# A hybrid attention layer on one core: the low part of the keys contracts over 64 rows instead of over 128 rows padded with zeros

## The chip, the cores and the metric

The kernel runs on one core of one Trainium2 chip. The metric is the device time of one execution in microseconds (us). TensorE is called PE below, its weight loads PEld, VectorE DVE, ScalarE ACT, GpSimd POOL and SyncE SP.

## What is computed

One decoder layer over 1024 tokens of width 2048, all in float32. A root-mean-square norm feeds one input projection of 6400 columns. Its columns go to two mixers:

```python
# A: 8 heads with two softmax maps each, head size 64, causal, value width 128
sc = einsum('bthcd,bshcd->bhcts', q, k) * 64 ** -0.5      # masked, softmax
a  = p[:, :, 0] - lam * p[:, :, 1]
oa = rmsnorm(einsum('bhts,bshe->bthe', a, v)) * (1 - lam_init) * silu(gate_a)
# B: 16 query heads, 2 key/value heads, window 128, a learned sink per head
ob = softmax([q k^T / 8 in the window, sink])[..., :-1] @ v * silu(gate_b)
out = x + concat(oa, ob) @ w_out
```

Queries and keys of both mixers get a norm per head and rotary angles first.

## The kernel before

**Precision.** Every product that must be close to float32 is made from two parts: a "hi" part, rounded to the matmul's own float32 format (F32R), and a "lo" part, the rest. The projection takes three matmuls for each tile (`three`, L854 to L856: hi·hi, hi·lo, lo·hi).

**Order of the work.** After a start of about 200 us (the norm of x, its transposes, the first two projected tiles) the kernel runs 13 units: 8 heads of A, 4 pairs of query heads of B, and a last one that drains. A unit has 16 steps of the same pattern, and every engine has its own hand-written program for a step (`body`), tied to the others by semaphores. In an even step PE does half a quarter of the next unit's projection (12 matmuls, 128x512), maybe transposes (L891), the second half of the quarter, then scores (`scores_a` with c = 0, or `scores_b`), and the transposes of the probabilities of the step before (L938). In an odd step it does the two halves of the projection with the transpose of an output between them (L974), `scores_a` with c = 1, the products with the values (L953, L955, or L966, L967 for B), and the transposes of the next queries and keys (L984). After the units comes the output projection (from 1640 us on).

**The scores.** A head's queries stand in `q_pair`: the 64 rows of one half (`half_rows[c]`) hold q hi, the 64 rows of the other half hold q lo. `k_dup[c]` holds k hi in both halves, so one matmul over all 128 rows, L897, gives q hi · k hi and q lo · k hi together. The second matmul, L898, adds q hi · k lo. It too runs over 128 rows: `kT_lo[c]` is a plane of its own for each c, with k lo in the half where q hi stands and zeros in the other. For A there are two such planes (planes 6 and 7 of `parts`, the tile called attention_parts in the trace). B uses plane 6 alone, with k lo in both halves, for both of its r; there the half with q hi is the upper one for r = 0 and the lower one for r = 1.

**The zeros.** POOL writes them once, at L1480, after it has made its share of the low part of x, and before the units begin PE waits for them (`k_zeros`). Each A step writes only the 64 rows of `kT_lo[c]` that hold k lo, so the zeros stay; B, which comes last, writes all rows of `kT_lo[0]` and needs none.

**Shapes.** For A and query block i, a map has (i+1)·128 keys, in pieces of at most 512: 1 piece for i below 4, 2 from 4 on. For B a step has 4 pieces of 256 (128 for i = 0). Each piece is one L897 and one L898, with the same 128 columns of `q_pair` as the weights.

**DMA.** All transfers of the trace but the one issued by ACT at the start come from SP's queue; POOL issues none.

Of the kernel before, what the change touches and what calls it, by code (L numbers as in the profile page):

```python
# [32 lines left out]
F32 = mybir.dt.float32  # L33
F32R = mybir.dt.float32r
I32 = mybir.dt.int32
ALU = mybir.AluOpType
# [3 lines left out]
P = 128  # L40
D = 2048
S = 1024
HD = 64
HALF = HD // 2
NR = S // P
# [119 lines left out]
def bank_of(name, first_it):  # L165
    return (BASE[first_it] + uses_of(first_it).index(name)) % 2


def qk_split(i, it, first):


    if i:
        return use_number(("T", i), it, first) + 1
    return BASE[first] + (it - first) * len(uses_of(first))
# [26 lines left out]
def decoder_layer(nc, x, positions, norm_w, w_in, q_norm_a, k_norm_a, lambda_q1, lambda_k1,  # L201
# [14 lines left out]
    with ExitStack() as ctx:  # L216
        def sb(name, shape, dt=F32):
            return ctx.enter_context(nc.sbuf_tensor(name, shape, dt))

        def sem(name):  # L220
            return ctx.enter_context(nc.semaphore(name))
# [9 lines left out]
        with nc.sbuf_tensor("x_raw_sb", [P, 3 * D + 2 * 512], F32) as x_raw_sb:  # L231
# [1 line left out]
            x_pieces = [x_raw_sb[:, 3 * D + j * 512:3 * D + (j + 1) * 512] for j in range(2)]  # L233


        parts = sb("attention_parts", [P, 8, S], F32R)
        k_dup = [parts[:, 0, :], parts[:, 1, :]]
        v_hi, v_lo = (parts[:, c, :].rearrange("p (n e) -> p n e", n=NR) for c in (2, 3))
        aT_hi, aT_lo = parts[:, 4, :], parts[:, 5, :]
        kT_lo = [parts[:, 6, :], parts[:, 7, :]]  # L240


        o_second_b = parts[0:HD, 1, 0:512]
# [2 lines left out]
        q_pair = sb("q_hi_lo", [P, 4 * P], F32R)  # L246
# [37 lines left out]
        p_tmp = ps_b[:, 3, :]  # L284
        half_rows = [slice(0, HD), slice(HD, P)]

        names = """consts k_zeros ident_ready par_in lam_in lam_sum lam_exp pos_in ang rope_arg rope_ready
            x_sq x_pow x_scaled x_hi norm_in
            w_hi_ready w_lo_ready w_used
            tp_done tp_free sq_ready ss_ready norm_chain rs_ready  # L290
# [3 lines left out]
        sm = {n: sem("s_" + n) for n in names}  # L294
# [5 lines left out]
        x_lo = {"dve": sem("s_x_lo_dve"), "pool": sem("s_x_lo_pool")}  # L300
# [25 lines left out]
        def wait(eng, s, value):  # L326

            if isinstance(value, int) and value <= 0:
                return
            eng.wait_ge(s, value)  # L330

        def iterations(eng, body, phases=PHASES):

            body(-1, -1)
            for f, n in phases:
                if n == 1:
                    body(f, f)
                else:
                    with eng.Fori(f, f + n) as it:
                        body(it, f)  # L340
# [510 lines left out]
        def _(pe):  # L851
            def three(dst, a_hi, a_lo, b_hi, b_lo, start, stop):

                pe.matmul(dst, a_hi, b_hi, start=start, stop=False)  # L854
                pe.matmul(dst, a_hi, b_lo, start=False, stop=False)  # L855
                return pe.matmul(dst, a_lo, b_hi, start=False, stop=stop)  # L856
# [30 lines left out]
            def turn_tile(d, b, n, bank):  # L887
                wait(pe, pp_copied[b], d["T"] + 1)
                bank_free(n)
                for r in range(4):  # L890
                    mm = pe.transpose(p_tr[bank][:, r * P:(r + 1) * P], stage[:, b, r * P:(r + 1) * P], ident[:, :])  # L891
                mm.then_inc(sm["tp_done"], 1)

            def q_times_k(dst, q, k, k_lo):


                pe.matmul(dst, q, k, start=True, stop=False)  # L897
                return pe.matmul(dst, q, k_lo, start=False, stop=True)  # L898

            def scores_a(st, c, it, first):  # L900
                i = st["i"]
                w = (i + 1) * P
                if c == 0:

                    wait(pe, sm["tp_free"], qk_split(i, it, first))
                wait(pe, sm["x_done"], st["G"] * 2 + c)
                flat = p_s.rearrange("p a b -> p (a b)")
                for lo in range(0, w, 512):
                    t = slice(lo, min(w, lo + 512))
                    mm = q_times_k(flat[:, t], q_pair[:, c * P:(c + 1) * P], k_dup[c][:, t], kT_lo[c][:, t])  # L910
                mm.then_inc(sm["s_done"], 1)

            def scores_b(st, it, first):
                i = st["i"]
                wait(pe, sm["tp_free"], qk_split(i, it, first))
                wait(pe, sm["x_done"], st["G"] * 2)
                t = slice(max(i - 1, 0) * P, (i + 1) * P)
                lo = P if i == 0 else 0
                for r in range(2):
                    for p in range(2):  # L920
                        mm = q_times_k(p_s[:, r, p * 256 + lo:p * 256 + 256],
                                       q_pair[:, (2 * r + p) * P:(2 * r + p + 1) * P], k_dup[0][:, t], kT_lo[0][:, t])
                    mm.then_inc(sm["s_done"], 1)

            def turn_probs(st, it, first):
# [88 lines left out]
            def body(it, first):  # L1014
                for s in range(16):
# [23 lines left out]
                    if s % 2 == 0:  # L1039
                        if cur and cur["k"] == "A":  # L1040
                            scores_a(cur, 0, it, first)
                        elif cur:
                            scores_b(cur, it, first)
                        if back1:
                            turn_probs(back1, it, first)
                        continue
                    if tb:
                        turn_tile(tb[0], tb[2], use_number(tb[1], it, first), bank_of(tb[1], first))
                    if cur and cur["k"] == "A":
                        scores_a(cur, 1, it, first)  # L1050
# [7 lines left out]
            def first_half_k(q, g):  # L1058

                if g == 0:  # L1060
                    pe.wait_ge(sm["w_lo_ready"], q + 1)
                if q == g == 0:
                    wait_x_lo(pe, 2 * NR - 4)
                    wait_x_lo(pe, 2 * NR - 1)
                w, kk = slice(g * P, (g + 1) * P), 4 * q + g
                return three(p_proj[0], w_hi[:, q, w], w_lo[:, q, w], hT_hi[:, kk, 0:512], hT_lo[:, kk, 0:512],
                             kk == 0, kk == KT - 1)

            pe.wait_ge(sm["ident_ready"], 2)
            for r in range(NR):  # L1070
                pe.wait_ge(sm["x_scaled"], r + 1)
                for g in range(4):
                    n = 4 * r + g
                    wait(pe, sm["tp_free"], n - 3)
                    for k in range(4):
                        f = (4 * g + k) * P
                        mm = pe.transpose(ps_b[:, g, k * P:(k + 1) * P], x_buf[r % 2][:, f:f + P], ident[:, :])
                    mm.then_inc(sm["tp_done"], 1)
                    q = r - NR // 2 - 1
                    if q >= 0:  # L1080
                        mm = first_half_k(q, g)
            for g in range(4):
                mm = first_half_k(3, g)
# [3 lines left out]
            for s in range(8):  # L1087
# [3 lines left out]
                quarter(KV_TILES[u], u, s % 4, 1, KV_TILES[0] if u else None)  # L1091
                if 4 <= s < 6:
                    turn_tile(KV_TILES[0], s - 4, 32 + s - 4, s % 2)
            pe.wait_ge(sm["k_zeros"], 2)
            iterations(pe, body)


# [4 lines left out]
            for r in range(4):  # L1102
                t = slice(512 + r * P, 512 + (r + 1) * P)
                for j in last:
                    k = OUT_TILES[j][1]
                    if r == 0:
                        pe.wait_ge(sm["w_lo_ready"], NQ_OUT + j + 1)
                    mm = three(ps_b[:, r, :], hT_hi[:, k, t], hT_lo[:, k, t], w_hi[:, j % 4, :], w_lo[:, j % 4, :],
                               j == last[0], j == last[-1])
# [4 lines left out]
        def _(dve):  # L1114
# [8 lines left out]
            def tt(o, a, b, op):  # L1123
                return dve.tensor_tensor(o, a, b, op)  # L1124
# [35 lines left out]
            ang = qkv[:, 1, 128:384]  # L1160
# [5 lines left out]
            left, parts = 2 * math.pi, []  # L1166
# [135 lines left out]
            def lo_qk(nk, i, it, first):  # L1302
                name = ("T", i)
                bank = p_tr[bank_of(name, first)]
                w = P if nk == "A" else 2 * P
                unit = it + 1 if i == 0 else it
                wait(dve, sm["t_hi"], (unit * NR + i) * 2 + 2)
                t = slice(i * P, (i + 1) * P)
                for c, h in enumerate(half_rows):
                    col = slice(c * w, (c + 1) * w)  # L1310
                    dve.scalar_tensor_tensor(q_pair[half_rows[1 - c], col], bank[h, 0:w], QSCALE,  # L1311
                                             q_pair[h, col].bitcast(F32), ALU.mult, ALU.subtract)
                if nk == "A":
                    for c, h in enumerate(half_rows):
                        ins = tt(kT_lo[c][h, t], bank[h, w:w + P], k_dup[c][h, t].bitcast(F32), ALU.subtract)
                else:
                    ins = tt(kT_lo[0][:, t], bank[:, w:w + P], k_dup[0][:, t].bitcast(F32), ALU.subtract)
                ins.then_inc(sm["tp_free"], 1)

            def combine(st):  # L1320
# [120 lines left out]
        def _(pool):  # L1441
# [32 lines left out]
                    if g == 1 and r + 2 < NR:  # L1474
                        x_rms(r + 2)

            pool.wait_ge(x_lo["dve"], NR)
            pool.wait_ge(x_lo["pool"], 3 * NR)
            for c in range(2):
                pool.memset(kT_lo[c][half_rows[1 - c], :].bitcast(F32), 0.0).then_inc(sm["k_zeros"], 1)  # L1480
                pool.wait_ge(sm["k_zeros"], c + 1)

            def norms(d, b):
                seq = d["K"] * 2 + b
                wait(pool, sm["ss_ready"], seq + 1)
                inv_rms(ss_h[:, 0:8], ss_h[:, 8:16], ss_h[:, 16:24], 2, sm["rs_ready"], seq * 3)
# [92 lines left out]
```

## Time and profile before

| | |
|---|---|
| Time, median of 3 runs (lowest, highest) | 1878.46 us (1877.18, 1879.02) |
| Time of the profiled execution | 1879.02 us |
| Span of its instructions | 1877.2 us |
| PE busy | 1807.0 us, 96% of the span |
| DVE, ACT, POOL busy | 59%, 43%, 23% |
| DMA | 98 GB/s over the span |
| Granted TensorE clock, mean | 0.993 of full speed |

The span runs from the first to the last instruction; 1.8 us of the profiled execution lie outside it. A matmul's row gives the start and a duration whose end is modelled, so the time that one matmul takes from the next is read from the distance of two starts and not from the duration. Weight loads have rows of their own (PEld) and can lie beside a matmul.

### The profile page before, as it was taken

What the parts mean: (1) busy time and instruction counts of PE and PEld (TensorE: products, weight loads), DVE (VectorE), ACT (ScalarE), POOL (GpSimd) and SP (SyncE); (2) the same over time, 40 slices, a digit from 0 to 9 for tenths busy, and PEclk for the clock granted to TensorE, in tenths of its full rate; (3) what the DMA queues carried; (4) which work ended last, traced back from release to release, by engine and by line L of the source; (5) the groups of instructions that cost most, each with busy time, mean ns of one, the idle gap of its engine ahead of it and who ended that gap; (6) DMA issues with size and microseconds to landing.
All of it is one profiled execution on the core that took longest, in us unless ns stands there. A gap on an engine that the chain in (4) does not pass through costs nothing.

```text
span 1877.2 us, 27880 instructions
## 1 busy us (share of the span) xinstructions
PE 1807.0 (96%) x8920; PEld 1507.0 (80%) x8920; DVE 1109.2 (59%) x2255; ACT 799.8 (43%) x2116; POOL 439.0 (23%) x664
## 2 busy tenths in 40 slices
PE   3899999999999999999999999999999889999999
PEld 3788878888788887888878888888888678788887
DVE  5734465665656657566575666758677866333333
ACT  5411354444544445444444444445444554222221
POOL 6512131322313223131231312313223521000000
PEclk9999999999999999999999999999999889999999
DMA  5122222222222222222222222323323544444445
GB/s 201 36 79 73 84 72 78 78 78 78 71 77 77 77 78 71 85 69 87 68 74 86 73 84 74 105 82 83 109 80 98 189 127 122 162 154 161 142 143 177
DMA packets 256504, 184.97 MB, mean 99 GB/s; under 512 B 31136, under 2 KB 227744, under 8 KB 255392
## 3 DMA queue, kind: packets, MB, share of 16 engines
q1 hardware_dynamic: 254352, 183.85, 32.3%
q8 instruction: 48, 0.79, 0.2%
q10 hardware_dynamic: 2064, 0.01, 0.1%
q14 instruction: 40, 0.33, 0.1%
HBM read 138.71 MB, written 45.09 MB: 98 GB/s over the span
## 4 chain that ended last, share of the span: by engine, by line
PE 79%; DVE 9%; issue 4%; DMA 3%; ACT 2%; POOL 2%; SPq 1%; DVEq 0%; ACTq 0%
PE ps_a L854 19%; PE ps_a L856 19%; PE ps_a L855 19%; PE ps_b L938 3%; PE ps_b L856 3%; PE ps_b L854 3%; PE ps_b L855 3%; PE ps_a L898 2%; DVE stage_rows L1124 2%; DMA qkv_sb<-qkv_a_dram 2%; PE ps_a L897 2%; PE ps_b L953 2%; PE ps_b L891 2%; PE ps_b L984 1%; DVE w_lo_sb L1124 1%
## 5 line engine op out<-in xcount | busy, mean ns | idle before, releaser
L854 PE MATMUL ps_a<-hT_hi,w_hi_sb 128*128 128x512 f32 x1696 | 694.1, 409 | 7.2 <-DVE stage_rows L1208 4.5
L856 PE MATMUL ps_a<-hT_hi,w_lo_sb 128*128 128x512 f32 x1696 | 667.4, 394 | 0.0
L855 PE MATMUL ps_a<-hT_lo,w_hi_sb 128*128 128x512 f32 x1696 | 664.1, 392 | 0.0
L1124 DVE TENSOR_TENSOR w_lo_sb<-w_raw_sb,w_hi_sb 128x512 fp32r<-128x512 f32 (+1 forms) x320 | 228.3, 716 | 272.1 <-ACT w_hi_sb L657 270.1
L856 PEld LDWEIGHTS ps_a<-hT_hi,w_lo_sb 128*128 128x128 f32 x1696 | 320.1, 189 | 71.8
L854 PEld LDWEIGHTS ps_a<-hT_hi,w_hi_sb 128*128 128x128 f32 x1696 | 321.2, 189 | 70.2 <-issue 7.2
L855 PEld LDWEIGHTS ps_a<-hT_lo,w_hi_sb 128*128 128x128 f32 x1696 | 321.8, 190 | 58.5
L657 ACT ACTIVATE w_hi_sb<-w_raw_sb 128x512 fp32r<-128x512 f32 (+1 forms) x320 | 197.8, 620 | 226.4 <-DMA w_raw_sb<-in_w_out 95.0
L817 ACT ACTIVATE expd<-ps_a,neg_max 128x256 f32<-128x256 f32 (+7 forms) x128 | 95.1, 743 | 213.3 <-DVE neg_max L1265 211.4
L749 ACT ACTIVATE attention_parts<-ps_b 128x512 fp32r<-128x512 f32 (+3 forms) x160 | 76.9, 521 | 224.2 <-PE ps_b L938 224.0
L1124 DVE TENSOR_TENSOR ps_a<-ps_a,mask 128x128 f32<-128x128 f32 (+2 forms) x192 | 77.5, 417 | 142.2 <-PE ps_a L898 140.8
L1459 POOL TENSOR_TENSOR ss_o<-ss_o,small 128x1 f32<-128x1 f32 x64 | 12.8, 201 | 560.8 <-ACT ps_b L773 560.8
L1124 DVE TENSOR_TENSOR attention_parts<-ps_b,attention_parts 64x128 fp32r<-64x128 f32 (+3 forms) x320 | 135.1, 439 | 7.6 <-ACT attention_parts L749 5.4
L1524 POOL TENSOR_TENSOR expd<-expd,inv_sum 128x1024 f32<-128x1024 f32 (+1 forms) x32 | 57.2, 1789 | 226.6 <-DVE inv_sum L1338 226.6
L897 PE MATMUL ps_a<-attention_parts,q_hi_lo 128*128 128x512 f32 (+2 forms) x320 | 99.1, 323 | 2.5 <-DVE attention_parts L1124 1.9
L1265 DVE TENSOR_REDUCE neg_max<-ps_a 128x1 f32<-128x256 f32 (+7 forms) x128 | 97.0, 758 | 4.4
L1311 DVE SCALAR_TENSOR_TENSOR q_hi_lo<-ps_b,q_hi_lo 64x128 fp32r<-64x128 f32 (+1 forms) x192 | 64.0, 333 | 59.3 <-ACT attention_parts L800 46.6
L1496 POOL TENSOR_TENSOR stage_rows<-stage_rows,ss_h 128x512 f32<-128x512 f32 x50 | 71.2, 1425 | 109.0 <-DVE stage_rows L1124 109.0
L898 PE MATMUL ps_a<-attention_parts,q_hi_lo 128*128 128x512 f32 (+2 forms) x320 | 95.6, 320 | 0.0
L854 PE MATMUL ps_a<-w_hi_sb,hT_hi 128*128 128x512 f32 x208 | 81.6, 392 | 3.4 <-DVE w_lo_sb L1124 2.9
L1463 POOL TENSOR_TENSOR ss_h<-ss_h,small 128x8 f32<-128x8 f32 x50 | 83.8, 1676 | 3.9
L856 PE MATMUL ps_a<-w_hi_sb,hT_lo 128*128 128x512 f32 x208 | 81.0, 389 | 0.0
(126 smaller groups left out, 2651.6 us busy)
## 6 DMA issues: line engine op xcount, KB each, us to landing
w_raw_sb<-in_w_in SPq DMA_DIRECT2D x200, 256.0 KB, 3.1
w_raw_sb<-in_w_out SPq DMA_DIRECT2D x104, 256.0 KB, 3.1
qkv_a_dram<-stage_rows SPq DMA_DIRECT2D x48, 256.0 KB, 2.4
qkv_sb<-qkv_a_dram SPq DMA_DIRECT2D x64, 192.0 KB, 3.0
x_raw_sb<-in_x SPq DMA_DIRECT2D x8, 1024.0 KB, 7.6
gates_dram<-stage_rows SPq DMA_DIRECT2D x32, 256.0 KB, 2.7
gate_y<-gates_dram SPq DMA_DIRECT2D x128, 64.0 KB, 2.4
y_dram<-gate_y SPq DMA_DIRECT2D x128, 64.0 KB, 2.3
```

What stands on the lines that cost most here:

```text
L657: act.activation(w_hi[:, b4, 0:w], w_raw[:, b4 % 2, 0:w], ACT.Copy).then_inc(sm["w_hi_ready"], 1)
L749: act.activation(aT_hi[:, lo:hi], p_tr[bank_of(name, first)][:, 0:hi - lo], ACT.Copy).then_inc(sm["at_hi"], 1)
L817: act.activation(expd[:, c, 0:w], flat[:, 0:w], ACT.Exp, bias=neg_max[:, c:c + 1], accum_out=sums[:, c:c + 1]).then_inc(sm["x_done"], 1)
L854: pe.matmul(dst, a_hi, b_hi, start=start, stop=False)
L855: pe.matmul(dst, a_hi, b_lo, start=False, stop=False)
L856: return pe.matmul(dst, a_lo, b_hi, start=False, stop=stop)
L897: pe.matmul(dst, q, k, start=True, stop=False)
L898: return pe.matmul(dst, q, k_lo, start=False, stop=True)
L1124: return dve.tensor_tensor(o, a, b, op)
L1265: dve.tensor_reduce(neg_max[:, c:c + 1], flat[:, 0:(i + 1) * P], AX, ALU.max, negate=True)\
L1463: pool.tensor_tensor(dst, mean, small[:, 0, 0:w], ALU.pow).then_inc(s, 1)
L1496: pool.tensor_tensor(x3, x3, ss_h[:, 16:24].unsqueeze(2).to_broadcast([P, 8, HD]), ALU.mult)\
```

## The change

1. `kT_lo` becomes one plane of 128 rows in place of two, with the k lo of c = 0 in the upper and of c = 1 in the lower half of the rows. `parts` has 7 planes instead of 8.
2. L898 contracts over the 64 rows of the half `h` alone: weights `q[h, :]`, moving operand `kT_lo[h, t]`. L897 stays as it is.
3. POOL's two memsets, their semaphore and PE's wait for it are gone.
4. The kernel is built with the default size of the descriptor scratch (16384 bytes of each partition in place of 4096).

```diff
-        parts = sb("attention_parts", [P, 8, S], F32R)
+        parts = sb("attention_parts", [P, 7, S], F32R)
-        kT_lo = [parts[:, 6, :], parts[:, 7, :]]
+        kT_lo = parts[:, 6, :]
...
-            def q_times_k(dst, q, k, k_lo):
+            def q_times_k(dst, q, k, h, k_lo):
                 pe.matmul(dst, q, k, start=True, stop=False)
-                return pe.matmul(dst, q, k_lo, start=False, stop=True)
+                return pe.matmul(dst, q[h, :], k_lo, start=False, stop=True)
...
+                h = slice(c * HD, (c + 1) * HD)
                 for lo in range(0, w, 512):
                     t = slice(lo, min(w, lo + 512))
-                    mm = q_times_k(flat[:, t], q_pair[:, c * P:(c + 1) * P], k_dup[c][:, t], kT_lo[c][:, t])
+                    mm = q_times_k(flat[:, t], q_pair[:, c * P:(c + 1) * P], k_dup[c][:, t], h, kT_lo[h, t])
...
                 for r in range(2):
+                    h = slice(r * HD, (r + 1) * HD)
                     for p in range(2):
                         mm = q_times_k(p_s[:, r, p * 256 + lo:p * 256 + 256],
-                                       q_pair[:, (2 * r + p) * P:(2 * r + p + 1) * P], k_dup[0][:, t], kT_lo[0][:, t])
+                                       q_pair[:, (2 * r + p) * P:(2 * r + p + 1) * P], k_dup[0][:, t], h, kT_lo[h, t])
...
-            pe.wait_ge(sm["k_zeros"], 2)
...
-                        ins = tt(kT_lo[c][h, t], bank[h, w:w + P], k_dup[c][h, t].bitcast(F32), ALU.subtract)
+                        ins = tt(kT_lo[h, t], bank[h, w:w + P], k_dup[c][h, t].bitcast(F32), ALU.subtract)
...
-            pool.wait_ge(x_lo["dve"], NR)
-            pool.wait_ge(x_lo["pool"], 3 * NR)
-            for c in range(2):
-                pool.memset(kT_lo[c][half_rows[1 - c], :].bitcast(F32), 0.0).then_inc(sm["k_zeros"], 1)
-                pool.wait_ge(sm["k_zeros"], c + 1)
...
-    nc = bacc.Bacc("TRN2", target_bir_lowering=False, num_devices=1, dynamic_dma_scratch_size=4096)
+    nc = bacc.Bacc("TRN2", target_bir_lowering=False, num_devices=1)
```

## Rows read from the trace of the kernel before

**Rows 1.** The page, part 1: busy time, share of the span, instructions.
```profile
PE 1807.0 (96%) x8920; PEld 1507.0 (80%) x8920; DVE 1109.2 (59%) x2255; ACT 799.8 (43%) x2116; POOL 439.0 (23%) x664
```

**Rows 2.** Busy time by stretch: stretch, length, each engine's busy time, granted clock, DMA share, GB/s.
```profile
203.00:1609.00 1406.00, 1376.37 (x6994) 1151.62 (x6993) 919.63 (x1975) 673.11 (x1916) 360.67 (x574) 0.99 0.30 87
```

**Rows 3.** PE's waits from 201 to 1609 us: us in total, times, longest.
```profile
PE ps_b L984 <- DMA qkv_sb<-qkv_a_dram: 7.1, 10, 1.0
PE ps_b L974 <- DVE attention_parts L1124: 5.4, 8, 0.8
...
PE ps_a L897 <- DVE attention_parts L1124: 1.9, 7, 0.4
```

**Rows 4.** The line L897: durations in ns, first and last start in us.
```profile
L897 PEld LDWEIGHTS ps_a<-attention_parts,q_hi_lo x320: 186/188/192, 201.3 to 1577.1; 128*128 128x128 f32 x160
```

**Rows 5.** Groups of the scores by shape: count, busy us, mean ns, idle before.
```profile
L897 PE MATMUL ps_a<-attention_parts,q_hi_lo 128*128 128x512 f32 x96 | 40.3, 420 | 2.5 <-DVE attention_parts L1124 1.9
L898 PE MATMUL ps_a<-attention_parts,q_hi_lo 128*128 128x512 f32 x96 | 37.5, 390 | 0.0
L898 PE MATMUL ps_a<-attention_parts,q_hi_lo 128*128 128x256 f32 x144 | 37.1, 283 | 0.0
L897 PE MATMUL ps_a<-attention_parts,q_hi_lo 128*128 128x256 f32 x144 | 36.7, 281 | 0.0
...
L898 PE MATMUL ps_a<-attention_parts,q_hi_lo 128*128 128x128 f32 x48 | 12.6, 276 | 0.0
L897 PE MATMUL ps_a<-attention_parts,q_hi_lo 128*128 128x384 f32 x32 | 11.4, 356 | 0.0
L898 PE MATMUL ps_a<-attention_parts,q_hi_lo 128*128 128x384 f32 x32 | 10.8, 338 | 0.0
L897 PE MATMUL ps_a<-attention_parts,q_hi_lo 128*128 128x128 f32 x48 | 10.6, 234 | 0.0
```

**Rows 6.** Timeline around one pair of 512 keys: start, duration, engine, line.
```profile
245.18 0.39 PE L856 MATMUL ps_a<-hT_hi,w_lo_sb 128*128 128x512 f32 x1
245.18 0.19 PEld L897 LDWEIGHTS ps_a<-attention_parts,q_hi_lo 128*128 128x128 f32 x1
...
245.41 0.39 PE L897 MATMUL ps_a<-attention_parts,q_hi_lo 128*128 128x512 f32 x1
245.41 0.19 PEld L898 LDWEIGHTS ps_a<-attention_parts,q_hi_lo 128*128 128x128 f32 x1
...
245.63 0.39 PE L898 MATMUL ps_a<-attention_parts,q_hi_lo 128*128 128x512 f32 x1
...
245.86 0.28 PE L953 MATMUL ps_b<-attention_parts 128*128 128x256 f32 x1
```

**Rows 7.** Timeline of PE around one pair of 128 keys.
```profile
254.30 0.22 PE L897 MATMUL ps_a<-attention_parts,q_hi_lo 128*128 128x128 f32 x1
254.36 0.28 PE L898 MATMUL ps_a<-attention_parts,q_hi_lo 128*128 128x128 f32 x1
254.47 0.63 PE L938 MATMUL ps_b<-ident,expd 128*128 128x128 f32 x4
```

**Rows 8.** Timeline of PE, then of PEld, where a pair follows transposes.
```profile
1077.74 0.60 PE L891 MATMUL ps_b<-ident,stage_rows 128*128 128x128 f32 x4
1078.09 0.47 PE L897 MATMUL ps_a<-attention_parts,q_hi_lo 128*128 128x512 f32 x1
1078.40 0.39 PE L898 MATMUL ps_a<-attention_parts,q_hi_lo 128*128 128x512 f32 x1
...
1078.06 0.19 PEld L897 LDWEIGHTS ps_a<-attention_parts,q_hi_lo 128*128 128x128 f32 x1
```

**Rows 9.** Timeline of POOL around the memsets.
```profile
71.17 1.99 POOL L1480 MEMSET attention_parts<- 64x1024 f32 x2
89.79 0.20 POOL L1459 TENSOR_TENSOR ss_h<-ss_h,small 128x8 f32<-128x8 f32 x1 [16.63 <-DVE ss_h L1227]
```

**Rows 10.** The page, part 4: the chain that ended last, shares by engine.
```profile
PE 79%; DVE 9%; issue 4%; DMA 3%; ACT 2%; POOL 2%; SPq 1%; DVEq 0%; ACTq 0%
```

More of the change, by code:

```diff
@@ L285, in decoder_layer @@
         half_rows = [slice(0, HD), slice(HD, P)]
-        names = """consts k_zeros ident_ready par_in lam_in lam_sum lam_exp pos_in ang rope_arg rope_ready
+        names = """consts ident_ready par_in lam_in lam_sum lam_exp pos_in ang rope_arg rope_ready
             x_sq x_pow x_scaled x_hi norm_in
@@ L1314, in lo_qk @@
                     for c, h in enumerate(half_rows):
-                        ins = tt(kT_lo[c][h, t], bank[h, w:w + P], k_dup[c][h, t].bitcast(F32), ALU.subtract)
+                        ins = tt(kT_lo[h, t], bank[h, w:w + P], k_dup[c][h, t].bitcast(F32), ALU.subtract)
                 else:
-                    ins = tt(kT_lo[0][:, t], bank[:, w:w + P], k_dup[0][:, t].bitcast(F32), ALU.subtract)
+                    ins = tt(kT_lo[:, t], bank[:, w:w + P], k_dup[0][:, t].bitcast(F32), ALU.subtract)
                 ins.then_inc(sm["tp_free"], 1)
```

## The prediction

> **What bounds the kernel now.** I read the page first, then the stages, then PE's waits, and last single instructions around the scores.
>
> The busy times say PE: 96% of the span, against 59% for the next engine [rows 1]. The chain of work that ended last gives PE 79% of its length [rows 10]. That is an average, so the stage in which the change acts counts: the scores run from 201 to 1577 us [rows 4], and from 203 to 1609 us PE is busy for 1376.4 of 1406.0 us [rows 2]. The list of PE's waits shows that little of the remaining 30 us is slack that longer scores could use up: 7.1 us for the rows of the next queries and keys, 5.4 us before the transposes of an output, 1.9 us before the scores themselves [rows 3]. So time that the scores add on PE is time of the kernel, nearly one for one, and other engines can be left aside: they have 35% of the time or more to spare in that stretch (DVE 919.6 of 1406.0 us) [rows 2].
>
> A busy PE is not one at its peak, so I looked at how two matmuls follow each other. The reader should see three things.
>
> First, a weight load is hidden now. The load for L898 starts at 245.41 us, in the moment in which the L897 before it starts, and L898 starts at 245.63: 0.22 to 0.23 us for each matmul of 512 columns, though each also needs a load whose row says 0.19 us [rows 6]. The load of the next weights lies beside the matmul that runs.
>
> Second, what a load costs where the matmul before it is too short to hide it. After an L897 of 128 columns L898 starts 0.06 us later, since its weights came in beside a longer matmul; but from that L898, of 128 columns as well, to the next start it is 0.11 us [rows 7]. A stream of 128-column matmuls is paced by the loads, at 0.11 us each. Four transposes in 0.35 us are the same thing (0.09 us each, the first load hidden) [rows 8].
>
> Third, what one load that isn't hidden costs a long matmul: the L897 behind four transposes has its load at 1078.06, only 0.03 us before its recorded start, and the next matmul starts 0.31 us after it, not 0.23 [rows 8]. 0.31 + 0.03 - 0.23 = 0.11 us: the same price by another row.
>
> **The change part by part.**
>
> *The memsets and the wait for them.* They take 1.99 us of POOL at 71.17 us, POOL has nothing else to do until 89.79 us, and PE needs the zeros only at 201 us [rows 4, 9]. The cover is 16.6 us on POOL's side and 128 us on PE's. Worth 0; if there were no cover it would be 2 us.
>
> *The descriptor scratch, and one plane fewer.* Tiles move to other addresses in their partitions, the shapes and the engines' partitions stay. All DMAs but one at the start come from SP's queue and none from POOL's. I found no row that would change; 0.
>
> *DVE's and ACT's part.* `lo_qk` writes the same two pieces of 64 rows, into one plane instead of two, with the same count of instructions and the same semaphores; 0.
>
> *L898 over 64 rows.* This is the change. L898 runs 320 times: 96 of 512 columns, 32 of 384, 144 of 256 and 48 of 128 [rows 5]. Its moving operand has as many columns as before, and a matmul is paced by its columns (0.23 us from start to start at 512 [rows 6]; at 384 and 256 the mean duration is 0.052 and 0.107 us less than at 512 [rows 5], so 0.18 and 0.12 us) or, at 128 columns, by the load behind it (0.11 us [rows 7]). Rows that carry zeros cost nothing there, so taking them away gives nothing: all rows of PE in this trace say 128*128, and none is of a contraction over 64.
>
> What it adds is that PE goes from a full array to half of the array's rows and back, for each piece. 320 pieces give 640 changes. No matmul, load or transpose in the trace of before is of another form, so what a change of form costs isn't shown, and I bound it. The lower end is 0: the load for the other form comes in beside the running matmul as it does now. The upper end is that PE lets the running matmul leave the array first and only then loads. A matmul's row lasts 0.39 us where the next starts 0.23 us later [rows 6], so 0.16 us of each lie beside the next one. Waiting for them and for the load makes 0.16 + 0.11 = 0.27 us for a change. Between them stands the row that is nearest to it, a load that is not taken ahead, at 0.11 us [rows 8]. I take that value, because the thing in doubt is whether the load of one form may lie beside a matmul of the other, and that row is the price of exactly this.
>
> The Trainium skill, page TensorEngine Tiling (Array Packing), section Key Properties, says that changing the tiling mode, as opposed to the tile within one mode, drains TensorE, and its section When to Use Tiling counts a contraction of 64 as a mode of its own. That rule speaks against this change; no row here shows it. The page TensorE: Matmul & The Clock Gate (section What happens when you issue a matmul) puts the last stretch of the wavefront at about 128 cycles, which at 2.4 GHz is 0.053 us; 640 of them would be 34 us, in place of the loads or on top of them (an estimate from these pages alone).
>
> The sum: where the piece has 256 columns or more (272 pieces) both changes of the pair expose the whole load, since it was wholly hidden: 2 x 272 x 0.11 = 59.8 us. Where it has 128 (48 pieces) half of a load was exposed already (0.11 between starts in place of 0.06 [rows 7]), so it is 2 x 48 x 0.055 = 5.3 us. Together 65.1 us. Against that goes slack: the wait for the rows of the next queries and keys falls in an odd step behind the scores [rows 3]. At 0.22 us a pair and two pairs ahead of it, about 0.4 us of a wait can be filled, 8 or so times: 3 us. What queues behind the longer pair on PE is all of PE's program; DVE's mask and maximum start 0.1 to 0.3 us later in a step of about 7.3 us (1406 us for 12 units of 16 steps) and their results are wanted a step later, so nothing else becomes late. Net +62 us. The profiled execution would go from 1879.02 to 1941 us; its time is 0.6 us above the median of the three runs, and so the median goes from 1878.46 to about 1940 us (+3.3%).
>
> **The rivals.**
>
> *The change of form is hidden (no change).* The load of 64 rows lies beside the full matmul, and the full load beside the half one, as now. For it: loads start in the same moment as the matmul before them throughout [rows 6], and leaving transposes, a different kind of work, costs no more than the load that the short matmul couldn't hide [rows 8]. Against it: all of these have one form, 128*128. The time is 1878.5 us: the memsets give nothing.
>
> *The array drains too.* Each change costs the tail and the load: 0.16 us more than in my sum, 640 x 0.16 = 102 us, in all 167 us less 3 us of slack: 2042 us. For it: 0.16 us of every row do lie beside the next matmul, so something is there to be waited for. Against it: the recorded ends are modelled and may overstate it. Half of the tail would give 1991 us.
>
> *It gets faster.* Only half of the array's rows are used by L898, and if a neighbour could run in the other half its time would vanish. By the distances above, L898's share is 96 x 0.23 + 32 x 0.18 + 144 x 0.12 + 48 x 0.11 = 50 us, so 1828 us at best. It decides from 3.8 us on, 0.012 us for a piece. Against it: both neighbours of each L898 use all 128 rows, and the L897 before it writes the same bank and the same columns. That a half load is quicker would show only at the 48 short pieces: 48 x 0.055 = 2.6 us, less than can be told.
>
> **How the numbers follow.** A measurement of this kernel tells no more than about 0.2% (3.8 us) from no change. My forecast, 0.03 to 0.15 us for a change of form (+19 to +96 us, less slack), gets 0.60; the drain with a tail on top, above 0.15 us, 0.24; the hidden change 0.13; faster 0.03. So slower 0.84, same 0.13, faster 0.03. The time is that of the forecast, 1940 us. The range goes from 1895 us (0.03 us a change) to 2020 us (0.23 us a change), and leaves out no change and faster (0.16) and the upper end of the draining case (about 0.04). The 0.27 us bound lies just above it.
>
> **What the profile after would show.** If I am right, L898's rows no longer say 128*128 but a form with 64; the load of L898 starts when the L897 before it has ended its columns and not with its start; from L897 to L898 and from L898 to the next start it is about 0.34 us at 512 columns in place of 0.23; PE's waits and the other engines' busy times stay within some us; and the stretches before 201 us and after 1609 us keep their lengths. If only the array's tail is waited for, the load still starts early and the distance grows by less than 0.11 us. If it is hidden, the distances stay 0.23. What would make me wrong is the size: the price of a change is the nearest row's and not its own, and 640 of them turn an error of 0.05 us into 32 us.

## The result and the profile after

The changed kernel takes 1971.14 us (median of 4 runs, 1969.64 to 1972.56) against 1877.82 us (4 runs) of the kernel before: a ratio of 1.0498 with a 95% interval of 1.0482 to 1.0512, or +93.3 us. The forecast was +62 us, with a range of 1895 to 2020 us.

The page's busy times, to be held against [rows 1]:

```profile
PE 1916.5 (97%) x8920; PEld 1521.5 (77%) x8920; DVE 1114.6 (57%) x2255; ACT 800.1 (41%) x2116; POOL 434.7 (22%) x662
```

The same number of matmuls and loads, 109.5 us more of busy PE, and at most 5.4 us of difference on the other engines. Busy time by stretch, to be held against [rows 2]; the first stretch is bounded at about the same work, 90 us later at its end, and the second one is what follows it:

```profile
203.00:1699.00 1496.00, 1482.74 (x6991) 1163.52 (x6990) 924.40 (x1974) 672.96 (x1914) 360.54 (x574) 1.00 0.28 82
1699.00:1968.60 269.60, 262.84 (x1150) 216.40 (x1148) 87.36 (x129) 59.91 (x94) 3.47 (x2) 0.99 0.47 157
```

The stretch with the scores has grown from 1406 to 1496 us and holds about the same counts of instructions; the granted clock in it is full. PE is idle for 13.3 us of it (1496.00 - 1482.74), where it was 29.6 us.

The scores by shape, to be held against [rows 5]:

```profile
L898 PE MATMUL ps_a<-attention_parts,q_hi_lo 64*128 64x256 f32 x144 | 54.9, 381 | 0.0
L897 PE MATMUL ps_a<-attention_parts,q_hi_lo 128*128 128x256 f32 x144 | 50.5, 351 | 0.0
L898 PE MATMUL ps_a<-attention_parts,q_hi_lo 64*128 64x512 f32 x96 | 47.6, 496 | 0.0
```

L898 now has the form 64*128, and its mean row is 0.10 us longer at either shape. The timelines of PE and then of PEld say what happens; before, a pair of 512 keys and a pair of 128 stood at [rows 6, 7]:

```profile
253.71 0.39 PE L856 MATMUL ps_a<-hT_hi,w_lo_sb 128*128 128x512 f32 x1
253.94 0.39 PE L897 MATMUL ps_a<-attention_parts,q_hi_lo 128*128 128x512 f32 x1
254.26 0.50 PE L898 MATMUL ps_a<-attention_parts,q_hi_lo 64*128 64x512 f32 x1
254.69 0.33 PE L897 MATMUL ps_a<-attention_parts,q_hi_lo 128*128 128x128 f32 x1
254.94 0.33 PE L898 MATMUL ps_a<-attention_parts,q_hi_lo 64*128 64x128 f32 x1
...
253.72 0.19 PEld L897 LDWEIGHTS ps_a<-attention_parts,q_hi_lo 128*128 128x128 f32 x1
254.26 0.18 PEld L898 LDWEIGHTS ps_a<-attention_parts,q_hi_lo 64*128 64x128 f32 x1 [0.35 <-issue]
254.69 0.19 PEld L897 LDWEIGHTS ps_a<-attention_parts,q_hi_lo 128*128 128x128 f32 x1 [0.25 <-issue]
254.94 0.18 PEld L898 LDWEIGHTS ps_a<-attention_parts,q_hi_lo 64*128 64x128 f32 x1
```

The load of L897 still starts with the L856 before it (253.72 beside 253.71). The load of L898 no longer starts with L897 at 253.94, but at 254.26, 0.32 us later, though the columns of L897 take 0.23. So PE waits about 0.09 us beyond the columns, and only then loads (a load that isn't hidden costs 0.11 us, [rows 8]). The same holds for the way back: from the load of L898 to the next load it is 0.43 us, which is 0.11 for the load, 0.22 for the columns, 0.10 on top. A matmul row that stands at the start of its own load (254.26, 254.69) contains that load, which is why the rows became longer.

Some of PE's waits between 203 and 1699 us, to be held against [rows 3]:

```profile
PE ps_b L986 <- DMA qkv_sb<-kv_b_dram: 2.2, 1, 2.2
PE ps_b L986 <- DMA qkv_sb<-qkv_a_dram: 1.3, 1, 1.3
PE ps_b L940 <- DVE stage_rows L1125: 1.0, 1, 1.0
```

L986 is the L984 of before: its wait for the rows of queries and keys went from 7.1 to 1.3 us, and the waits before the output's transpose (5.4 us) and before the scores (1.9 us) are gone from the list. Over the whole kernel PE is idle for 52.1 us (span less busy time), where it was 70.2 us.

### The profile page after: what moved, and what is told of

It reads as the page before. It is cut to its first block, busy times and chain, and to the rows that moved or that the text cites. A ratio compares the mean times of both kernels' runs of the same rounds, so it can differ in the third digit from the quotient of the medians.

```text
span 1968.6 us, 27876 instructions
## 1 busy us (share of the span) xinstructions
PE 1916.5 (97%) x8920; PEld 1521.5 (77%) x8920; DVE 1114.6 (57%) x2255; ACT 800.1 (41%) x2116; POOL 434.7 (22%) x662
## 4 chain that ended last, share of the span: by engine, by line
PE 88%; DVE 4%; DMA 2%; issue 2%; ACT 2%; POOL 1%; SPq 1%; DVEq 0%; ACTq 0%
PE ps_a L854 20%; PE ps_a L856 20%; PE ps_a L855 20%; PE ps_a L898 5%; PE ps_a L897 4%; PE ps_b L940 3%; PE ps_b L955 3%; PE ps_b L855 2%; PE ps_b L856 2%; PE ps_b L854 2%; PE ps_b L891 2%; PE ps_b L986 1%; DMA qkv_sb<-qkv_a_dram 1%; PE ps_b L957 1%; DVE stage_rows L1125 1%
## 5 line engine op out<-in xcount | busy, mean ns | idle before, releaser
L856 PE MATMUL ps_a<-hT_hi,w_lo_sb 128*128 128x512 f32 x1696 | 666.3, 393 | 0.0
L856 PEld LDWEIGHTS ps_a<-hT_hi,w_lo_sb 128*128 128x128 f32 x1696 | 319.7, 189 | 71.6
L898 PE MATMUL ps_a<-attention_parts,q_hi_lo 64*128 64x512 f32 (+2 forms) x320 | 132.0, 413 | 0.0
L897 PE MATMUL ps_a<-attention_parts,q_hi_lo 128*128 128x512 f32 (+2 forms) x320 | 118.3, 370 | 0.1
L898 PEld LDWEIGHTS ps_a<-attention_parts,q_hi_lo 64*128 64x128 f32 x320 | 58.5, 183 | 65.5 <-issue 50.7
L897 PEld LDWEIGHTS ps_a<-attention_parts,q_hi_lo 128*128 128x128 f32 x320 | 59.8, 187 | 34.6 <-issue 17.4
```

The costliest lines, as they stand in the source:

```text
L898: return pe.matmul(dst, q[h, :], k_lo, start=False, stop=True)
```

## The experiments

The theory: the price is that of PE changing between matmuls over 128 and over 64 rows, about 0.20 us of PE each, whatever is computed. Its rivals: the loss comes from something else in the change (addresses, scratch, memsets); it is a price of each 64-row matmul; it is peculiar to the scores.

**One part alone, and all the rest.** `e1_rows_only` is the kernel before with

```diff
-                return pe.matmul(dst, q, k_lo, start=False, stop=True)
+                return pe.matmul(dst, q[h, :], k_lo, start=False, stop=True)
```

and the 64 rows `h` of `kT_lo[c]` in its calls.

> The kernel before with one edit: L898 contracts over the 64 rows of its half; the two planes, their zeros, the wait and the scratch size stay. Theory (the price is that of PE changing between 128 and 64 rows, 640 times): all of the loss is here, 1971 us (+93). Rival (the loss comes from the tiles' new addresses or the scratch): 1878 us.

Measured: 1972.85 us against 1879.46, ratio 1.0500 (1.0483 to 1.0516).

`e2_rest_only` is the changed kernel with that line turned back (and `kT_lo[:, t]`).

> The changed kernel, but L898 contracts over all 128 rows again, of the one plane without zeros; this adds a product of q lo with the other map's k lo to the scores of A, and of q lo with k lo to those of B. Theory (rows alone): 1878 us, within 0.2%, as the memsets, the wait, the addresses and the scratch are worth nothing. Rival (addresses or scratch): well above 1878 us, up to 1971.

Measured: 1879.73 us against 1879.46, ratio 1.000 (0.9991 to 1.0009). The whole loss comes from the rows of L898; memsets, wait, plane and scratch together are worth less than 0.1%.

**Other orders of the same matmuls.** `e3_grouped` is the changed kernel with

```diff
+                for t in ts:
+                    pe.matmul(flat[:, t], q, k_dup[c][:, t], start=True, stop=False)
+                for t in ts:
+                    mm = pe.matmul(flat[:, t], q[h, :], kT_lo[h, t], start=False, stop=True)
...
```

for A, and for B, per p, both L897 (r = 0, 1) and then both L898. `e4_grouped_b` has B's part alone.

> The changed kernel with the same matmuls in another order: all L897 pieces of an A call first, then its L898 pieces; in B the L897 of both r, then the L898 of both r. 384 changes of form instead of 640, 320 matmuls of 64 rows as before. Theory (price per change, 0.20 us on PE, 0.146 us net of slack): 256 changes fewer give 37 to 51 us back, 1920 to 1934 us. Rival (price per 64-row matmul, 0.29 us each): 1971 us. If the two L898 of B, which use different halves of the array, also run beside each other, up to 7 us more comes back.

> As the grouped order, in B alone; 512 changes. Theory (price per change): 19 to 26 us back, 1945 to 1952 us, and if L898s of different halves run beside each other their starts stand under 0.05 us apart and another 7 us comes back. Rival (price per 64-row matmul): 1971 us.

Measured: 1923.85 us (ratio 1.0246, 1.0230 to 1.0261) and 1945.93 us (1.0357, 1.0341 to 1.0373). With 320 matmuls over 64 rows in all three kernels, the loss is 93, 66 and 44 us for 640, 512 and 384 changes. That rules out a price of each 64-row matmul alone. In a B step of `e4_grouped_b` the two L898 are not one after the other. Timeline of PE:

```profile
1433.59 0.40 PE L926 MATMUL ps_a<-attention_parts,q_hi_lo 128*128 128x256 f32 x2
1433.92 0.39 PE L930 MATMUL ps_a<-attention_parts,q_hi_lo 64*128 64x256 f32 x2
1434.23 0.50 PE L926 MATMUL ps_a<-attention_parts,q_hi_lo 128*128 128x256 f32 x2
```

Two matmuls of 256 columns with the wait and the load take 0.31 us (1433.92 to 1434.23), as one did in the changed kernel (there 0.31 us from an L898 of 256 columns to the next). Over the 56 such pairs of the run it is 0.315 us on average. The two use different halves of the rows and write different banks of PSUM, the memory that matmuls write to.

`e11_grouped_b_same_half` is `e4_grouped_b` with both in one half:

```diff
-                        h = half_rows[r]
+                        h = half_rows[0]
```

> The grouped order in B alone (which took 1946 us), but the L898 of both r use the same half of the rows; for r = 1 that half of q_pair holds q lo, so its score gets q lo x k lo in place of q hi x k lo. The same 512 changes. Theory (L898s of different halves run beside each other, those of one half one after the other): 64 pairs x 0.12 us slower, 1952 to 1954 us, and a pair of 256 columns takes about 0.43 us in place of 0.31. Rival (the halves make no difference): 1946 us.

Measured: 1949.10 us, ratio 1.0370 (1.0356 to 1.0384). The forecast of 1952 to 1954 us was missed: this is 3 us above `e4_grouped_b`, and the intervals overlap, so the times confirm no price of the same half. The rows are clear; timeline of PE:

```profile
1452.14 0.50 PE L930 MATMUL ps_a<-attention_parts,q_hi_lo 64*128 64x256 f32 x2
1452.57 0.50 PE L926 MATMUL ps_a<-attention_parts,q_hi_lo 128*128 128x256 f32 x2
```

The same two take 0.43 us now, 0.12 us more, and so do all 56 pairs (0.429 us on average).

**Both matmuls over 64 rows.** `e5_both_64`:

```diff
-                pe.matmul(dst, q, k, start=True, stop=False)
+                pe.matmul(dst, q[h, :], k[h, :], start=True, stop=False)
```

> The changed kernel, but L897 contracts over the same 64 rows as L898 too; the product q lo with k hi is left out. 640 matmuls of 64 rows, but only 320 changes of form (in and out of each call). Theory (price per change): half of the loss, 1920 to 1930 us, if one 64-row load hides behind a 64-row matmul. If a load of the same form and the same rows does not hide, 0.1 us more for each of the 320 inner steps, 1955 us. Rival (price per 64-row matmul): 1878 + 640 x 0.29 - slack, about 2050 us.

Measured: 1908.04 us, ratio 1.0153 (1.0137 to 1.0170): 29 us for 320 changes and 640 matmuls over 64 rows, so the forecast of 1920 to 1930 us (42 to 52 us) was missed. In A it is as expected; timeline of PE in an A step:

```profile
247.16 0.39 PE L856 MATMUL ps_a<-hT_hi,w_lo_sb 128*128 128x512 f32 x1
247.48 0.50 PE L897 MATMUL ps_a<-attention_parts,q_hi_lo 64*128 64x512 f32 x1
247.82 0.39 PE L898 MATMUL ps_a<-attention_parts,q_hi_lo 64*128 64x512 f32 x1
248.14 0.39 PE L955 MATMUL ps_b<-attention_parts 128*128 128x256 f32 x1
```

0.32 us into the 64-row form, 0.34 with the load that was not taken ahead, and 0.32 out of it; from then on loads are ahead again (a second 64-row matmul in the same form has no load of its own to wait for). In B a step was faster than before: in 28 of its 32 steps 1.00 us from the start of L856 to the transposes, where the kernel before has 1.18. Two more runs looked at this alone: `e12_b_both_64` is the kernel before, A untouched, with both matmuls of B over the 64 rows of half r; `e13_b_both_64_same_half` has half 0 for both r.

```diff
+                        h = half_rows[r]
...
-                                       q_pair[:, (2 * r + p) * P:(2 * r + p + 1) * P], k_dup[0][:, t], kT_lo[0][:, t])
+                                       q_pair[h, (2 * r + p) * P:(2 * r + p + 1) * P], k_dup[0][h, t], kT_lo[0][h, t])
```

> The kernel before with A untouched; in B both L897 and L898 contract over the 64 rows of their half r, and the product q lo x k hi is left out. 64 changes of form, two in a step. Theory (matmuls of the two halves run beside each other, also out of program order, so that a step's eight take 0.68 us with both changes in place of 0.96): 32 steps x about 0.2 us faster, 1872 to 1875 us. Rival (only the price of the changes counts): 64 x 0.20 = 13 us slower less slack, 1885 to 1891 us.

> As the run with both matmuls of B over 64 rows, but all eight of a step use the same half of the rows; for r = 1 that half holds q lo, so its scores are of q lo alone. Theory (no neighbour in the other half, so eight matmuls one after the other at 0.12 us plus both changes): 32 x 0.4 us = 13 us slower less slack, 1885 to 1891 us. Rival (the gain of the other run came from fewer rows and not from the halves): 1872 to 1875 us.

Measured: 1877.93 us (ratio 0.9991, 0.9982 to 1.0000) and 1888.66 us (1.0045, 1.0032 to 1.0059). Timelines of PE in a B step, first of `e12_b_both_64`:

```profile
1303.68 0.39 PE L856 MATMUL ps_a<-hT_hi,w_lo_sb 128*128 128x512 f32 x1
1304.00 0.40 PE L897 MATMUL ps_a<-attention_parts,q_hi_lo 64*128 64x256 f32 x2
1304.22 0.29 PE L898 MATMUL ps_a<-attention_parts,q_hi_lo 64*128 64x256 f32 x2
1304.34 0.29 PE L897 MATMUL ps_a<-attention_parts,q_hi_lo 64*128 64x256 f32 x2
1304.46 0.29 PE L898 MATMUL ps_a<-attention_parts,q_hi_lo 64*128 64x256 f32 x2
1304.68 1.09 PE L939 MATMUL ps_b<-ident,expd 128*128 128x128 f32 x8
```

then of `e13_b_both_64_same_half`, its ends:

```profile
1308.01 0.39 PE L856 MATMUL ps_a<-hT_hi,w_lo_sb 128*128 128x512 f32 x1
1308.33 0.38 PE L897 MATMUL ps_a<-attention_parts,q_hi_lo 64*128 64x256 f32 x1
...
1309.26 0.28 PE L898 MATMUL ps_a<-attention_parts,q_hi_lo 64*128 64x256 f32 x1
1309.46 1.09 PE L939 MATMUL ps_b<-ident,expd 128*128 128x128 f32 x8
```

With the halves apart, from L856 to the transposes it is 1.00 us, with one half 1.45 us. The kernel before took 1.18 us there (a step of its trace runs from 1303.25 to 1304.43 us), and these times hold in 28 of the 32 steps of each run. In the first fence two L897 start together, then two L898, although the program has L897, L898, L897, L898 for r = 0 and then the same for r = 1: the four matmuls of the one half ran beside the four of the other. So in `e13` the direction and the size are the theory's (+9.3 us). In `e12` only the rows show the gain of 0.18 us a step, which would be 6 us; the time shows 1.4 us, at the edge of nothing, and the forecast of 1872 to 1875 us was missed. The 0.18 us leave out a part of the change back that lies behind them: from the first transpose to the second it is 0.165 us in place of 0.112 on average (the load of the first is no longer taken ahead), 1.7 us for 32 steps. Waits of PE for the next queries and keys were 8.8 us in place of 7.1. That leaves about 2 us, against the 1.4 measured. The product left out in these runs would need a third 64-row matmul for each piece, so this is no faster kernel.

**Away from the scores.** The kernel before, with the scores untouched, and in each of the 428 half quarters of the projection one 512-column matmul over fewer rows (`n = slice(0, 64 if k == 0 else P)`, also with 96 and with 32), or the three of one k tile (`if k == 1`):

```diff
-                    mm = three(p_proj[b], w_hi[:, q, w], w_lo[:, q, w], hT_hi[:, kk, t], hT_lo[:, kk, t],
-                               kk == 0, kk == 4 * nk - 1)
...
+                    pe.matmul(p_proj[b], a_hi, b_hi, start=kk == 0, stop=False)
+                    pe.matmul(p_proj[b], a_hi[n, :], b_lo[n, :], start=False, stop=False)
+                    mm = pe.matmul(p_proj[b], a_lo, b_hi, start=False, stop=kk == 4 * nk - 1)
```

> The kernel before, scores untouched. In each of the 428 half quarters of the projection one matmul of 512 columns (hi x lo of the first k tile) contracts over rows 0 to 63; the other half of that product is left out. 856 changes. Theory (price per change 0.20 us on PE): + 171 us less up to 20 us of slack, 2028 to 2050 us. Rival (the price is peculiar to the scores, where both matmuls read the same weights from q_pair): 1878 us.

> As the run with one 64-row matmul in a half quarter, but all three of one k tile, in a row, contract over rows 0 to 63; half of that k tile's product is left out. 856 changes again, three times as many 64-row matmuls. Theory (price per change): the same 2028 to 2050 us. Rival (price per 64-row matmul, 0.39 us): about 2360 us.

> As the run with one 64-row matmul in a half quarter, but over 96 rows; the rows left out are 96 to 127. Theory (what counts is the form of the array in the row, and 96 rows still need the full one): 1878 us. Rival (any count under 128 has the price): 2028 to 2050 us.

> As the run with one 64-row matmul in a half quarter (which took 2020 us, +142), but over 32 rows; three quarters of that product are left out. Theory (the price is a fixed one for leaving and re-entering the full form, whichever the other form is): 2020 us again, and the same 0.43 us from start to start. Rival (the tail that is waited for grows with the rows in use): less by up to 856 x 0.05 = 43 us.

| run | 64-row (or other) matmuls | changes | us | ratio to before |
|---|---|---|---|---|
| e6_proj_one_64 | 428 | 856 | 2020.31 | 1.0745 (1.0727 to 1.0763) |
| e7_proj_three_64 | 1284 | 856 | 2031.69 | 1.0816 (1.0798 to 1.0834) |
| e8_proj_one_96 | 428 of 96 rows | see text | 1883.16 | 1.0023 (1.0013 to 1.0032) |
| e9_proj_one_32 | 428 of 32 rows | 856 | 2021.77 | 1.0754 (1.0737 to 1.0770) |

Three times the 64-row matmuls cost 11 us more, not 334 (856 more of them at 0.39 us): the price is that of the change, not of the matmul. The forecast of 2028 to 2050 us was met by `e7` and missed by 8 us by `e6`: there the distances around the 64-row matmul grew by 0.39 us for each half quarter (0.088 before it, 0.197 from it and 0.104 behind it, on average), 167 us in all, of which 141 came out at the end. Timeline of PE in `e7_proj_three_64`:

```profile
299.23 0.40 PE L856 MATMUL ps_a<-hT_hi,w_lo_sb 128*128 128x512 f32 x1
299.56 0.50 PE L854 MATMUL ps_a<-hT_hi,w_hi_sb 64*128 64x512 f32 x1
299.90 0.40 PE L855 MATMUL ps_a<-hT_lo,w_hi_sb 64*128 64x512 f32 x1
300.14 0.39 PE L856 MATMUL ps_a<-hT_hi,w_lo_sb 64*128 64x512 f32 x1
300.46 0.50 PE L854 MATMUL ps_a<-hT_hi,w_hi_sb 128*128 128x512 f32 x1
300.80 0.40 PE L855 MATMUL ps_a<-hT_lo,w_hi_sb 128*128 128x512 f32 x1
```

0.33 and 0.34 us at the one change, 0.32 and 0.34 at the other, 0.24 between two of the same form: each change is 0.20 us over twice 0.23. With 32 rows the price is the same; timeline of PE in `e9_proj_one_32`:

```profile
303.59 0.50 PE L883 MATMUL ps_a<-hT_lo,w_hi_sb 32*128 32x512 f32 x1
304.02 0.50 PE L884 MATMUL ps_a<-hT_hi,w_lo_sb 128*128 128x512 f32 x1
```

With 96 rows there is no such price in the rows (0.24 us from start to start); timeline of PE in `e8_proj_one_96`:

```profile
302.48 0.40 PE L883 MATMUL ps_a<-hT_lo,w_hi_sb 96*128 96x512 f32 x1
302.72 0.40 PE L884 MATMUL ps_a<-hT_hi,w_lo_sb 128*128 128x512 f32 x1
```

So it isn't any count of rows under 128; a matmul over 96 rows behaves like one in the full form. The run is slower by 4.2 us, more than its interval. A part stands in the rows: from a 96-row matmul to the next start it is 0.235 us on average, where the matmul in its place has 0.231 in the kernel before, 1.9 us for 428 of them (one trace of each). The rest stays open.

## Why the prediction was right, and where it was off

**What bounds the kernel.** Right in kind: work added on PE between 203 and 1609 us came out at the end. "Nearly one for one" was too strong: of 115 us added, 91 came out (below).

**The parts at nothing.** Right: memsets, wait, plane, scratch together 0.3 us (`e2_rest_only`), which is not told from nothing, and the one line alone gives all of the loss (`e1_rows_only`).

**The price of a change.** This term was mis-sized. I took 0.11 us, a load that isn't taken ahead. What the trace shows is that load and a wait of about 0.10 us before it, 0.20 us where a load had been wholly hidden. That the wait is for the array to empty is the likely reading; the rows show the wait and not what is waited for. The wait does not depend on the columns: from an L898 to the next start it is on average 0.43, 0.37, 0.31 and 0.25 us at 512, 384, 256 and 128 columns; less 0.11 for the load and 0.21, 0.16, 0.11 and 0.05 for the columns (0.107 us for each 256 [rows 5]) that leaves 0.09 to 0.11 at each of them. By its mechanism the rival that the array drains too was right, with a tail nearer to 0.10 than to the 0.16 us that it read from the ends of rows. At 0.18 us on average (the sum below) a change also costs more than the 0.15 us up to which the forecast's case went; the price lies in the case that had a chance of 0.24.

The Trainium skill, page TensorEngine Tiling (Array Packing), section Key Properties, says that changing the tiling mode drains TensorE; the traces agree, with a wait of 0.09 to 0.11 us before the load of the other form. The Trainium skill, page TensorE: Matmul & The Clock Gate, section What happens when you issue a matmul, gives about 128 cycles (0.053 us at 2.4 GHz) for the last stretch of the wavefront. That is about half of the measured wait; the measurement decides.

**The sum.** I added up the distances between consecutive PE starts, by pair of lines, over the timelines of both kernels. Those from L897 to L898 went from 51 to 96 us, those from L898 to what follows from 50 to 110 us, and those behind the next matmul, which now starts at its own load, grew by 11 us (46.7 to 52.5 behind L953, 10.2 to 15.1 behind the first transpose of the probabilities). That is 115 us of cost, 0.18 us for each of 640 changes, where I had 65. Small pieces take it below 0.20, as I had foreseen for the 48 of 128 columns.

**Slack.** Also mis-sized, the other way. I had 3 us, for the first of the three waits that I had listed and for none of the other two. All distances together grew by 91.3 us, as the spans of the two traces did (1968.6 - 1877.2 = 91.4; the medians differ by 93.3), so those that did not hold the 115 us shrank by 24 us: 6.8 before the output's transposes, 5.8 before the transposes of queries and keys, 4.5 before the scores, 1.8 in one long wait within the transposes of the probabilities, and the rest in small ones. PE's idle time fell by only 18.1 us of these, because a wait shorter than the modelled tail of the matmul before it isn't idle time there. Two errors of opposite sign, 50 us in the price and 21 us in the slack, made the forecast look better than its price was; that the time lies so far inside the range is in part luck.

**The rivals.** The hidden change of form was wrong at every change looked at. Faster was wrong for this kernel, but its mechanism exists: two halves do run beside each other. Both neighbours of each L898 use all the rows, as I argued, and nothing of it was seen here; where I gave the half arrays no chance to work together, a different order shows it (`e4_grouped_b`, `e12_b_both_64`).

**What the profile would show.** L898 with a form of 64 rows, its load later than the start of L897, the other engines nearly unmoved and the ends of the kernel of about the same length (201.5 and 200.0 us to the first of the scores, 299.9 and 301.6 us from the last one to the end): seen. PE's waits did not stay as they were; that is the slack above. The distances were forecast as 0.34 us each; they are 0.32 and 0.43, and the matmul behind them, which starts at its own load, takes up to 0.11 more: together 0.20 us for a change and not 0.11.

## What to carry to other kernels

What follows was measured with F32R operands, weights of 128 columns and the full granted clock. Padding a contraction of 64 rows with zeros to the 128 of its neighbours costs nothing where the columns set the pace (0.23 us for 512 columns over 128 rows, 0.24 over 64 in `e7_proj_three_64`), and taking the padding away costs about 0.2 us for each change of form, so count changes and not small matmuls: put matmuls of one form together, or leave them all in the full form. A gain from a half-row form was seen only where both halves had work at the same time, in different banks (one bank for both was not tried), and in `e12_b_both_64` four matmuls for each half were just about enough for the two changes. When slack is estimated, add up the distances between starts; waits that lie beneath the modelled end of a matmul are not in the list of waits.

## What the runs showed of the hardware that I had not expected

Matmuls over different halves of the rows that write different banks ran beside each other even where the program has three matmuls of the one half between them: a B step of `e12_b_both_64` took 1.00 us instead of 1.45 in `e13_b_both_64_same_half`, with starts in pairs about 0.01 us apart. A change of form costs the same with 32 rows as with 64 (2021.77 and 2020.31 us), and 96 rows have no such price (1883.16 us). Within the 64-row form a load is taken ahead as in the full form, for the same half too (0.24 us from start to start in `e7_proj_three_64`).
